# Expert choice by pairwise comparisons, and router logits with tokens on partitions, in a two-layer transformer kernel

## The reference

```python
def _grouped_moe(x, router_w, router_b, w_gate, w_up, w_down):
    t = x.reshape(b * s, d)
    scores = jax.nn.sigmoid((t @ router_w).astype(jnp.float32))
    sel = scores + router_b.astype(jnp.float32)
    grouped = sel.reshape(-1, N_GROUPS, N_EXPERTS // N_GROUPS)        # 8 groups of 4
    group_score = jnp.sum(lax.top_k(grouped, 2)[0], axis=-1)
    group_mask = jnp.argmax(group_score, axis=-1)[:, None] == jnp.arange(N_GROUPS)[None, :]
    in_group = jnp.where(group_mask[:, :, None], grouped, -jnp.inf).reshape(-1, N_EXPERTS)
    _, idx = lax.top_k(in_group, TOP_K)                               # 2 experts of the best group
    gate = jnp.take_along_axis(scores, idx, axis=-1)
    gate = gate / jnp.sum(gate, axis=-1, keepdims=True)
    combine = jnp.sum(jax.nn.one_hot(idx, N_EXPERTS) * gate[..., None], axis=1)
    y = jnp.zeros_like(t)
    for e in range(N_EXPERTS):
        h = jax.nn.silu(t @ w_gate[e]) * (t @ w_up[e])
        y = y + combine[:, e:e + 1] * (h @ w_down[e])
```

## Time and profile before

| what | value |
|---|---|
| median of 3 runs | 724.19 us (722.73 to 724.41) |
| the profiled execution | 722.91 us, its span 721.1 us |
| busy share of the span | PE 94%, DVE 46%, ACT 29%, POOL 18% |
| granted TensorE clock, mean | 0.987 of full speed |
| DMA | 237.66 MB, mean 330 GB/s |

### The profile page before, as it was taken

How to read it: one execution, slowest core, us unless ns; L and a number is a source line. 1 busy time by engine, 2 the same in 40 slices (tenths; PEclk the granted TensorE clock), 3 DMA queues, 4 the chain that set the end, 5 groups by cost and what they waited for, 6 DMA issues and landing times.

```text
span 721.1 us, 9996 instructions
## 1 busy us (share of the span) xinstructions
PE 679.4 (94%) x3617; PEld 384.5 (53%) x3617; DVE 331.2 (46%) x679; ACT 212.4 (29%) x416; POOL 129.6 (18%) x143
## 2 busy tenths in 40 slices
PE   7999999889999999999989898988999999999993
PEld 5879878463343343435546776846333334333551
DVE  4658755743434233242274755674343423323226
ACT  4558660421111111111155145342111211112112
POOL 4004010152110010100029560015211101010000
PEclk9999999999999999999999999999999999999997
DMA  8990049959999999999995019385999999999991
GB/s 304 381 357 2 1 187 402 372 204 359 425 421 422 422 420 422 422 422 422 423 413 202 0 44 422 126 349 215 360 424 421 421 421 422 422 422 422 420 404 62
DMA packets 40168, 237.66 MB, mean 330 GB/s; under 512 B 3824, under 2 KB 4000, under 8 KB 15040
## 3 DMA queue, kind: packets, MB, share of 16 engines
q1 hardware_dynamic: 39120, 235.37, 80.1%
q10 hardware_dynamic: 576, 1.05, 0.4%
q0 software_dynamic: 432, 0.70, 0.4%
HBM read 236.06 MB, written 1.05 MB: 329 GB/s over the span
## 4 chain that ended last, share of the span: by engine, by line
PE 88%; DVE 7%; issue 2%; ACT 2%; POOL 1%; POOLq 0%; DVEq 0%; ACTq 0%
PE psum L562 85%; PE psum L1022 2%; POOL scratch L2182 1%; DVE ln_stats L1616 1%; DVE work L1953 1%; DVE work L431 1%; PE psum L872 1%; ACT scratch L1471 0%; PE psum L577 0%; PE psum L657 0%; DVE x_T L1581 0%; POOLq L2166 0%; DVE scratch L1906 0%; DVE ring_rounded L1687 0%; DVE small L1909 0%
## 5 line engine op out<-in xcount | busy, mean ns | idle before, releaser
L562 PE MATMUL psum<-ring,work 128*64 128x512 f32 (+2 forms) x1296 | 231.3, 506 | 3.9 <-DVE work L2047 3.9
L562 PEld LDWEIGHTS psum<-ring,work 128*64 128x64 f32 (+1 forms) x1296 | 94.3, 138 | 137.9 <-issue 116.8
L562 PE MATMUL psum<-ring,scratch 128*64 128x512 f32 x512 | 116.9, 598 | 3.7 <-ACT scratch L1471 3.7
L2089 DVE TENSOR_TENSOR scratch<-psum,scratch 128x256 f32<-128x256 f32 x32 | 13.6, 425 | 183.2 <-ACT scratch L1467 183.2
L2167 POOL COPY work<-work 128x512 f32 x60 | 37.4, 626 | 302.5 <-PE psum L562 295.8
L1460 ACT ACTIVATE x_T_rounded<-psum,small 128x512 fp32r<-128x512 f32 x64 | 43.8, 688 | 110.1 <-DVE scratch_rounded L2070 75.7
L562 PEld LDWEIGHTS psum<-ring,scratch 128*64 128x64 f32 x512 | 33.9, 136 | 68.8 <-issue 63.6
L1467 ACT ACTIVATE scratch<-psum 128x256 f32<-128x256 f32 x32 | 12.3, 384 | 195.1 <-PE psum L562 195.1
L562 PE MATMUL psum<-ring_rounded 128*128 128x256 f32 (+1 forms) x214 | 66.1, 309 | 0.0
L562 PE MATMUL psum<-x_T_rounded,scratch_rounded 128*128 128x512 f32 x144 | 63.1, 438 | 1.9 <-ACT x_T_rounded L1460 1.4
L562 PE MATMUL psum<-ring_rounded,x_T_rounded 128*128 128x512 f32 x192 | 60.7, 397 | 0.0
(11 more groups left out here) (265 smaller groups left out, 850.0 us busy)
## 6 DMA issues: line engine op xcount, KB each, us to landing
ring<-in_moe_w_gate SPq DMA_DIRECT2D x64, 1024.0 KB, 15.6
ring<-in_moe_w_up SPq DMA_DIRECT2D x64, 1024.0 KB, 19.6
ring<-in_moe_w_down SPq DMA_DIRECT2D x64, 1024.0 KB, 20.6
ring<-in_diff_w_qkv SPq DMA_DIRECT2D x5, 2048.0 KB, 19.5
ring<-in_diff_w_o SPq DMA_DIRECT2D x1, 4096.0 KB, 15.7
ring<-in_mla_w_o SPq DMA_DIRECT2D x1, 4096.0 KB, 35.3
ring<-in_mla_w_q_b SPq DMA_DIRECT2D x1, 2304.0 KB, 28.9
ring<-in_mla_w_kv_b SPq DMA_DIRECT2D x1, 2048.0 KB, 27.8
```

The lines of the kernel that those rows point to most:

```text
L562: return pe.matmul(dst, lhsT, rhs, start=start, stop=stop, skip_group_check=True)
L2089: dve.tensor_tensor(h_sb, psum[:, 6, FF:2 * FF], act_s, ALU.mult).then_inc(m["h_ready"], 1)
```

## The change

The edits are, with both layers alike:

- The row product moves from behind the transposes into the last attention product, ahead of `out_part(1, 1)`; VectorE copies it and makes tile 0's offset before its last `add`.
- The logits are made with tokens on partitions: for each tile eight products with `x_T` as weights (128 columns) and 32 moving columns of router weights. The copy to `logit_T` and the two `fold` products go.
- Three of the four copies to `x_T` are ScalarE's, one VectorE's. ScalarE normalises both tiles behind the sigmoid.
- The choice compares the four experts of each group in pairs (`beaten`, 3 results an expert, 192 values), sums them to a place (0 = best), and takes the two with place under 2; group score, `chosen` and the one-hot rows `oh` come from the places. The two rounds of maxima over 32 experts go.
- The fillers `keep_clock(TOP_WAIT)` come right behind the logits. Tile 0's remainders stay ahead of `m_ready`, tile 1's move behind the rank products, with 2 fillers instead of 8 behind them. The sort waits for `tok_lo` tile by tile, and once more at the bank that the remainders used.

```diff
-ROW_BANK = (6, 3)
+ROW_BANK = (3, 7)
+LOGIT_BANK = 1
-START_WAIT, FIRST_WAIT, NORM_WAIT, TOP_WAIT, SORT_WAIT = 14, 8, (11, 0), 6, 8
+START_WAIT, FIRST_WAIT, NORM_WAIT, TOP_WAIT, SORT_WAIT = 14, 8, (11, 0), 6, 2
...
# TensorE
+            def row_product(l):
+                pe.wait_ge(z_ready, TT * l + 1)
+                mm(psum[:, ROW_BANK[l], 0:2 * EXPERTS], ones, routing()["rows"], True, True).then_inc(mo[l]["lg_ps"], 1)
...
+                        if (t, c) == (1, 1):
+                            row_product(0)
                         out_part(t, c, range(4, HEADS)).then_inc(wo_ps, 1)
...
-                mm(psum[:, ROW_BANK[l], 0:2 * EXPERTS], ones, routing()["rows"], True, True).then_inc(m["lg_ps"], 1)
-                pe.wait_ge(*x_copied(2 * l + 1))
-                for k in range(KD):
-                    rows = slice((k % 4) * EXPERTS, (k % 4 + 1) * EXPERTS)
-                    last = mm(psum[rows, 0, 0:SEQ], rw_scaled[:, k, :], xT[:, k, :], k < 4, k >= 4)
-                last.then_inc(m["lg_ps"], 1)
-                pe.wait_ge(*m("router_act", 1))
-                for t in range(TT):
-                    last = mm(psum[:, 1, t * EXPERTS:(t + 1) * EXPERTS], logit_T[:, t * P:(t + 1) * P], fold, True, True)
-                last.then_inc(m["lg_ps"], 1)
-                pe.wait_ge(cast_ready, 3)
-                for t in range(TT):
+                def logits(t):
+                    for k in range(KD):
+                        last = mm(psum[:, LOGIT_BANK, t * EXPERTS:(t + 1) * EXPERTS], xT[:, k, t * P:(t + 1) * P],
+                                  rw_scaled[:, k, :], k == 0, k == KD - 1)
+                    last.then_inc(m["lg_ps"], 1)
+                def remainders(t):
                     banks = [psum[:, REST_BANK[t] + c, :] for c in range(2)]
...
+                pe.wait_ge(*m("router_act", 1))
+                logits(0)
+                pe.wait_ge(*x_copied(2 * l + 1))
+                logits(1)
+                pe.wait_ge(cast_ready, 3)
                 keep_clock(TOP_WAIT, 0)
+                remainders(0)
                 pe.wait_ge(*m("m_ready", 1))
...
                 mm(rank[:, 96:128], ones_b[:, :], chosen[:, 0, :], False, True).then_inc(m["rank_ps"], 1)
+                remainders(1)
                 keep_clock(SORT_WAIT, 0)
...
# ScalarE
                 root(n, 0)
-                raw_copy(0)
+                raw_copy(0, 0)
+                raw_copy(0, 1).then_inc(m["router_act"], 1)
+                raw_copy(1, 0).then_inc(xt[n + 1]["sb"], KD // 2)
                 root(n, 1)
-                raw_copy(1)
                 act.activation(small[:, 60:61], eps[:, :], ACT.Sigmoid)
-                act.wait_ge(*m("lg_ps", 2))
-                act.copy(logit_T, psum[:, 0, 0:SEQ]).then_inc(m["router_act"], 1)
-                normalise(0)
                 act.wait_ge(*m("logit", TT))
                 act.activation(routing()["score"], routing()["sel"], ACT.Sigmoid).then_inc(m["router_act"], 1)
+                act.wait_ge(*xt[n + 1]("ps", 4))
+                normalise(0)
                 normalise(1)
...
# VectorE
-                tt(mx2, quad[:, :, 0::2], quad[:, :, 1::2], ALU.max)
-                tt(sm2, quad[:, :, 0::2], quad[:, :, 1::2], ALU.add)
-                tt(c["t1"], mx2[:, :, 0], mx2[:, :, 1], ALU.add)
-                tt(c["t2"], sm2[:, :, 0], sm2[:, :, 1], ALU.max)
-                tt(c["gs"], c["t1"], c["t2"], ALU.max)
+                dve.tensor_tensor(beaten[:, :, 0::2, 0], quad[:, :, 1::2], quad[:, :, 0::2], ALU.is_gt)
+                dve.tensor_tensor(beaten[:, :, 1::2, 0], quad[:, :, 0::2], quad[:, :, 1::2], ALU.is_ge)
+                dve.tensor_tensor(beaten[:, :, 0:2, 1:3], rivals(2), own(0), ALU.is_gt)
+                tt(beaten[:, :, 2:4, 1:3], rivals(0), own(2), ALU.is_ge)
+                chain(dve.tensor_reduce(place, beaten, AX.X, ALU.add))
+                chain(dve.scalar_tensor_tensor(out=two, in0=place, scalar=2.0, in1=quad, op0=ALU.is_lt, op1=ALU.mult))
+                chain(dve.tensor_reduce(c["gs"], two, AX.X, ALU.add))
...
-                chain(dve.tensor_scalar(c["gmask"], c["gmask"], 1.0, BIG, ALU.subtract, ALU.mult))
-                tt(masked, quad, c["gmask"].unsqueeze(2).broadcast_to(wide), ALU.add)
+                in_group = c["gmask"].unsqueeze(2).broadcast_to([P, TT * GROUPS, PER_GROUP])
+                dve.scalar_tensor_tensor(out=c["chosen"].rearrange("p t (g e) -> p (t g) e", e=PER_GROUP), in0=place,
+                                         scalar=2.0, in1=in_group, op0=ALU.is_lt, op1=ALU.mult).then_inc(m["m_ready"], 1)
                 for j in range(2):
-                    chain(dve.tensor_reduce(c["m1"], te(c["masked"]), AX.X, ALU.max))
-                    tt(te(c["e1"]), te(c["masked"]), spread(c["m1"], EXPERTS), ALU.is_equal)
-                    tt(te(c["e1"]), te(c["e1"]), per_tile(w32, EXPERTS), ALU.mult)
-                    chain(dve.tensor_reduce(c["k1"], te(c["e1"]), AX.X, ALU.max))
-                    tt(oh[:, j], te(c["e1"]), spread(c["k1"], EXPERTS), ALU.is_equal)
...
+                    last = dve.scalar_tensor_tensor(
+                        out=c["oh"][:, j * both:(j + 1) * both].rearrange("p (g e) -> p g e", e=PER_GROUP), in0=place,
+                        scalar=float(j), in1=in_group, op0=ALU.is_equal, op1=ALU.mult)
+                chain(last)
```

94 lines of the change are left out of this document (44 added, 50 removed).

## The result

| kernel | median | executions | ratio to before, 95% interval |
|---|---|---|---|
| before | 723.58 us | 5 (721.99 to 724.41) | 1 |
| changed | 718.17 us | 5 (716.38 to 719.64) | 0.992 [0.9898, 0.9942] |

The change made the kernel 5.4 us faster. Over all executions, those of the later experiments too, the mean of before is 723.34 us (117 executions, one of 3652 us in a later run left out) and of the changed kernel 718.31 (21), a difference of 5.0 +- 0.55. The profiled execution of the changed kernel took 716.38 us, its span 714.5.

What follows compares the result with a forecast made beforehand. TensorE was taken to bound the kernel, with routing savings reaching the end. Second layer +0.65 - 2.1 + 0.4 = -1.05 us, first -1.65, together -2.7: 720.2 from the profiled execution, 721.5 from the median; 720.8 taken, range 718.6 to 723.2.

Steps and rivals of the forecast that it cites:

- What bounds the kernel: TensorE holds 88% of the chain of waits; expert loop full and untouched, so what the routing saves, the end saves.
- Row product: Moved into the attention product: two passes put 0.22 us ahead of the transposes; its copy and tile 0's offset cost nothing.
- Logits: First transpose to logits: 32 passes 0.112 us apart put the first logit at 476.1 instead of 475.43, losing 0.65 us.
- rival of slow loads: Logits' weight loads don't overlap: from 0.156 us a pass the gain is eaten; at 0.19, 725.6 us; chance 0.06.
- cheap passes: Logits' passes at 0.08 us apart: each layer gains 1.0 us more, 718.8 us; chance 0.07.
- The choice: VectorE, bias add to copy of the counts: 4.75 to 4.95 us against 7.04, a gain of 2.1 us.
- The stall: In VectorE's choice, GpSimd's rounding holds the two-operand step behind the 192-value reduce: 0.65 us, bounds 0 and 1.03.
- The comparisons with repeated operands: Rival in VectorE's choice: comparisons and stall at upper bounds, 0.3 + 0.4 us a layer, 722.2 us; chance 0.10.
- TensorE in time: Ahead of the rank products: TensorE free 3.4 us behind the bias add, `m_ready` at 3.9; 0.7 us late does no harm.
- The clock's rival: TensorE's clock falls in both layers' routing, TensorE 1.0 us behind `m_ready`: 0.3 to 0.5 us a layer, 721.6; chance 0.17.
- Behind the ranks: Counts to sort: tile 1's remainders and two fillers put the sort at 3.5 us, 0.4 later than its data.
- First layer: Same as the second layer, plus 0.6 us counted for the old clock fall no longer paid: -1.65 us.

Runs made afterwards that it cites:

- choice alone: Kernel before with only the new pairwise choice on VectorE, nothing else changed: 720.83 us against 723.38, ratio 0.9967.
- old choice: Changed kernel with the old choice on VectorE put back, all else as changed: 724.42 us against 723.38, ratio 1.0016.
- padded: Changed kernel plus seven unused VectorE additions a routing, fillers behind the logits raised from six: with 13, 723.94 us (ratio 1.0016); with 16, 723.40 us (1.000).
- fillers moved: Kernel before with its six fillers moved from behind both tiles' identity products to right behind the fold products: 725.97 us against 723.57, ratio 1.0027.

## Why the prediction was too small

- *What bounds the kernel.* Right as far as shown: a routing made longer comes out at the end (5.3 us for 5.8), and the loop's windows are as before. That nothing else saves is not shown.
- *Row product.* Forecast 0.22 us, found 0.14. Its copy and offset lie between VectorE's last adds and cost nothing.
- *Logits.* Right: a loss, at the pace of passes with the same weight shape. Found 0.109 us a pass against 0.112; the first pass came 1.95 us behind the first transpose, so the stage ends 0.34 us later than before where 0.43 was forecast (0.65 with the row product). The rival of slow loads (0.156 us and more) and that of cheap passes (0.08) are both out.
- *The choice.* Forecast a gain of 2.1 us, found 2.26 in the layer without a fall. The comparisons were too dear: without waits they start 0.10 to 0.14 us apart (I had 0.2). The stall was too cheap, 0.8 us (0.65), and from the start of `chosen` to the pick 0.53 us pass (I had 0.46, which leaves out the step of `chosen` itself). These cancel: the working's own sum, 4.1 + 0.65 = 4.75 us to the counts, was right to 0.03. The 2.1 us are the cautious end of its 4.75 to 4.95, and that is what was lost here. The reduce (472.90 to 473.25) was all but over when the rounding began, so that it might be held was not tried here. The comparisons with repeated operands took 0.22 us like plain ones, so that rival is out.
- *TensorE in time.* Forecast free 0.5 us ahead of `m_ready`, found 0.28 where the clock held, and 0.4 late where it fell, which the forecast's cover of 0.7 took up. The clock's rival named the event (two of six routings) and mispriced it: TensorE 1.0 us behind `m_ready` and 0.3 to 0.5 us a layer forecast, 0.4 late and nothing lost found. The fall came under fillers, and behind these stand 0.71 us of waiting for the normalised tile (133.96), which took up part of it.
- *Behind the ranks.* Forecast 0.4 us, found 0.2.
- *First layer.* Forecast 0.6 us for a fall that would not be paid again, found 0.6 (7.66 against 7.04). That this fall is there in one of four profiled routings of before, and not each time, the sum did not ask.

The step that failed is the sum: three of its terms were too pessimistic. In the second layer -1.05 us was forecast and 1.71 - 0.14 = 1.57 found, nearly 0.2 each from the logits with the row product, from the choice and from the sort's wait. That makes 3.8 us on these profiles instead of 2.7. It would have moved the forecast from 720.8 to 719.7, still inside the range; what put the time below it is a part that no term of the sum holds. Over all profiles of the two kernels (before 16.86, 16.26, 16.25, 16.25; changed six times 14.5) the routings hold 2 x (16.40 - 14.54) - 0.28 = 3.4 us, while the means of the executions differ by 5.0 +- 0.55. The prediction took one profile's difference for that of the executions.

Where the missing 1.5 us lie stays open, and with it why the time fell below the range. Some 0.2 of it is outside the span: an execution takes 2.1 us more than its span in the mean of before and 1.9 in the changed kernel. Fewer falls are not it: the mean granted clock is 0.987 in both, over 112 and 21 executions. That each fall costs the kernel before more is likelier, but not shown. What is shown is that a fall is dear where TensorE is late or stood idle ahead of the ranks (choice alone, old choice, padded, fillers moved), and over the executions a microsecond taken by the clock, span x (1 - mean clock), goes with 0.75 +- 0.11 us more span in before and 0.39 +- 0.15 in the changed kernel. But no profile shows where: one of the four profiled routings of before had a fall, at 0.6 us. The rival, a steady saving outside the routings, is not excluded either.

## What to carry to other kernels

Shortening one engine's work between two products pays only as far as the other engine's queue is out of the way: with the new choice alone the order let through 1.1 us of 2.3 in the layer where the clock held, and nothing in the other. Put fillers where a fall of the clock passes under them with a wait behind, and not under products that something waits for. Price small VectorE instructions without waits by the distance of their starts, and let the range hold all terms being off the same way: three of 0.2 us in two layers were half of its lower side.

## What the runs showed of the hardware

- A VectorE instruction with two SBUF operands is held by GpSimd's rounding of 128x1024 values until 0.03 to 0.08 us behind its end (1.03 us instead of 0.23; 0.46 instead of 0.17), both where it starts 0.08 us into the rounding and where it starts 0.6 us into it. Reduces of 16 and 64 values inside the rounding were not (0.17 and 0.22 us), nor was a two-operand step that had begun 0.12 us ahead of it (134.50, 0.23 us).
- Passes with float32 weights of 128 columns and 32 moving columns run 0.109 us apart over 32 passes, 0.28 us each.
- Behind idle stretches of 0.93 to 3.03 us four float32 identity products of 512 columns took 3.31 to 3.76 us in seven routings; at full clock 1.88 to 1.98. Behind one of 2.28 us they took 1.96, and behind 0.89 us eight fillers ran at full speed (1.89).
- Comparisons with stepped and repeated operands of 32 to 64 values: 0.21 to 0.22 us; contiguous steps of 64 values take 0.23.
